# A separate choice for head 0, and an earlier start for GpSimd's gathers

## The reference

```
q = (xc @ w_q).reshape(PEER_CHUNK, PEER_HEADS, PEER_DKEY)      # 128 tokens, 8 heads, 256
s1 = q[..., :128] . keys1;  s2 = q[..., 128:] . keys2          # 128 keys each
v1, i1 = top_k(s1, 16);  v2, i2 = top_k(s2, 16)
cand = v1[:, None] + v2[None, :];  sv, si = top_k(cand, 16)
idx = e1 * 128 + e2                                            # 16 experts of 16384
g = softmax(sv)
a = gelu(u_tab[idx] . xc)
out = sum over heads and k of (g * a) * v_tab[idx]
```

## Time and profile before

| what | value |
|---|---|
| runs | 2523.37 us median of 3 (2520.69 to 2524.76) |
| profiled execution | 2523.2 us |
| its span, first to last instruction | 2521.4 us |
| VectorE, GpSimd, TensorE busy | 1533.2, 1488.0, 1406.7 us |
| read from HBM | 936.46 MB |
| the gathers' share of the 16 DMA engines | 80.7% |
| mean granted TensorE clock | 0.741 of full speed |

### The profile page before, as it was taken

One profiled execution on the slowest core, in us unless ns is written; L12 is line 12 of the kernel. 1 busy time (PEld: TensorE's weight loads), 2 busy tenths in 40 slices (PEclk: granted clock), 3 DMA queues, 4 the chain that ended last, 5 costly groups with the idle time before them and its releaser, 6 DMA issues.

```text
span 2521.4 us, 22041 instructions
## 1 busy us (share of the span) xinstructions
PE 1406.7 (56%) x7198; PEld 633.2 (25%) x7198; DVE 1533.2 (61%) x3968; ACT 344.2 (14%) x695; POOL 1488.0 (59%) x1546
## 2 busy tenths in 40 slices
PE   7897775455674665345435433369657546434333
PEld 3446521123331432011011110026434224101000
DVE  1244867877955675766776554414769755687542
ACT  2221210122301111010001000014113111000000
POOL 0001666776776567776777667610366766677773
PEclk9898887677797877667555765679869778665566
DMA  9824999999999999999999999993799999999997
GB/s 346 313 100 180 391 406 407 409 407 374 407 394 408 405 404 407 409 409 407 406 409 409 403 402 409 385 342 121 291 406 409 406 407 405 409 393 409 410 409 269
DMA packets 287856, 939.02 MB, mean 372 GB/s; under 512 B 27760, under 2 KB 28544, under 8 KB 287488
## 3 DMA queue, kind: packets, MB, share of 16 engines
q0 software_dynamic: 221184, 805.40, 80.7%
q1 hardware_dynamic: 66560, 132.21, 14.2%
HBM read 936.46 MB, written 1.05 MB: 372 GB/s over the span
## 4 chain that ended last, share of the span: by engine, by line
DMA 30%; POOL 25%; PE 24%; issue 10%; DVE 8%; ACT 2%; SPq 0%; DVEq 0%; POOLq 0%; ACTq 0%
POOL RING L720 25%; DMA RING<-in_p_v,IDV 22%; PE acc L1281 7%; DMA RING<-in_p_u,IDX 6%; PE wk L1482 5%; DVE RING L804 3%; PE wk L1343 3%; PE wk L1467 2%; PE wk L1310 1%; PE wk L1267 1%; PE wk L1320 1%; DMA WR<-in_o_w_in 1%; DVE STM L972 1%; PE wk L1426 1%; DMA WR<-in_ada_w 1%
## 5 line engine op out<-in xcount | busy, mean ns | idle before, releaser
L804 DVE SCALAR_TENSOR_TENSOR RING<-RING,acc 128x1024 f32<-128x1024 f32 x768 | 916.0, 1219 | 496.5 <-DMA RING<-in_p_u,IDX 453.4
L1281 PE MATMUL acc<-RING,ST 128*32 128x512 f32 x3072 | 604.2, 927 | 944.8 <-DMA RING<-in_p_v,IDV 942.6
L720 POOL DMA_INDIRECT RING<-in_p_u,IDX x768 | 740.3, 964 | 621.0 <-DVE WG L1072 348.2
L720 POOL DMA_INDIRECT RING<-in_p_v,IDV x768 | 746.1, 972 | 394.2 <-issue 206.8
L1281 PEld LDWEIGHTS acc<-RING,ST 128*32 128x32 f32 x3072 | 118.8, 145 | 1330.5 <-issue 1318.3
L1482 PE MATMUL wk<-HT,WR 128*128 128x256 f32 (+1 forms) x832 | 158.1, 349 | 13.1 <-DMA WR<-in_p_w_q 12.4
L1482 PEld LDWEIGHTS wk<-HT,WR 128*128 128x128 f32 x832 | 138.8, 197 | 37.6 <-issue 22.3
L1240 ACT ACTIVATE GA<-A 128x16 f32<-128x16 f32 x48 | 10.3, 215 | 739.6 <-DVE RING L804 739.5
L1343 PE MATMUL wk<-WR,HT 128*128 128x512 f32 x232 | 106.2, 614 | 2.5 <-DMA WR<-in_o_w_in 2.5
L1514 PE MATMUL wk<-SELW,WE 128*128 128x512 f32 x96 | 70.6, 825 | 41.0 <-DVE WE L825 41.0
L1242 ACT ACTIVATE ST<-wk 128x512 f32<-128x512 f32 x48 | 28.7, 597 | 375.1 <-PE wk L1514 375.1
(11 more groups left out here) (189 smaller groups left out, 1637.5 us busy)
## 6 DMA issues: line engine op xcount, KB each, us to landing
WR<-in_p_w_q SPq DMA_DIRECT2D x25, 1024.0 KB, 11.8
WR<-in_ada_w SPq DMA_DIRECT2D x23, 1024.0 KB, 11.3
RING<-in_ada_w SPq DMA_DIRECT2D x23, 1024.0 KB, 13.6
RING<-in_p_u,IDX POOLq DMA_INDIRECT x768, 11.9
RING<-in_p_v,IDV POOLq DMA_INDIRECT x768, 11.9
WR<-in_o_w_in SPq DMA_DIRECT2D x11, 1024.0 KB, 15.7
WR<-in_e_w_in SPq DMA_DIRECT2D x8, 1024.0 KB, 15.6
WR<-in_o_w_out SPq DMA_DIRECT2D x5, 1024.0 KB, 12.5
```

Of the source, the lines that this page charges most:

```text
L720: pool.indirect_dma_start(out=ring[:, n % NU, :], out_offset=None, in_=tables[table], in_offset=bass.IndirectOffsetOnAxis(ap=rows, axis=0) ...
L804: nc.vector.scalar_tensor_tensor(out=U[:, s % NU, :], in0=U[:, s % NU, :], scalar=1.0, in1=acc[:, 1, :], op0=ALU.mult, op1=ALU.mult, accum ...
L1281: ins = nc.tensor.matmul(acc[32 * g:32 * g + 32, 0, hf * 512:hf * 512 + 512], ST[:, c % 2, s, :], V[:, s % NV, hf * 512:hf * 512 + 512], s ...
```

## The change

HEAD_FIRST becomes true. The front of each layer now scores head 0, makes the "xin" transposes, makes all three parts of head 0's choice, scores head 1, makes parts 0 and 1 of its choice, scores heads 2 and 3, and goes on as before. Part 2 of head 1's choice comes after the first four products, its "ixT" one step later and its "ixD" two. The parts of the choice of (2, 3) come one step later each. GpSimd waits for a new semaphore, indexed, which the cast to IDX releases, and the cast now stands ahead of the expansion and of the wait for the exponential.

```diff
--- before.py
+++ after.py
@@ -56,7 +56,7 @@
 PAIR01 = 9
 ORDER = ((2, 3, 0, 1), (0, 1))
 ALONE = (False, True)
-HEAD_FIRST = False
+HEAD_FIRST = True
 
 
 def units(l):
@@ -135,7 +135,9 @@
     t = ORDER[l][0]
     heads = choices(l, t)[0]
     s = [("score", l, tiles, heads), ("xin", l, t), *[("topk", l, t, heads, p) for p in range(3)]]
-    return s + [("score", l, tiles, (1,))] * HEAD_FIRST + [("score", l, tiles, (2, 3)), *then]
+    if HEAD_FIRST:
+        s += [("score", l, tiles, (1,)), ("topk", l, t, (1,), 0), ("topk", l, t, (1,), 1)]
+    return s + [("score", l, tiles, (2, 3)), *then]
 
 
 def next_choices(f, l, t):
@@ -144,11 +146,10 @@
     put(f, 0, ("ixT", l, t, heads[0]))
     put(f, 1, ("ixD", l, t, heads[0]))
     if HEAD_FIRST:
-        put(f, 0, ("topk", l, t, (1,), 0), ("topk", l, t, (1,), 1))
-        put(f, 1, ("topk", l, t, (1,), 2))
-        put(f, 2, ("ixT", l, t, (1,)))
-        put(f, 3, ("ixD", l, t, (1,)))
-        choose(f, l, t, (2, 3), (2, 3, 4, 5, 6))
+        put(f, 0, ("topk", l, t, (1,), 2))
+        put(f, 1, ("ixT", l, t, (1,)))
+        put(f, 2, ("ixD", l, t, (1,)))
+        choose(f, l, t, (2, 3), (1, 2, 3, 4, 5))
     else:
         choose(f, l, t, (2, 3), (0, 1, 2, 3, 4))
 
@@ -567,6 +568,7 @@
         topks = [s[:4] for s in named("topk") if s[4] == 0]
         shifted = Count(sem("shifted"), topks)
         texp = Count(sem("texp"), topks)
+        indexed = Count(sem("indexed"), topks)
         chosen = Count(sem("chosen"), topks)
         scores_used = Count(sem("scores_used"), topks)
         u_in = [sem(f"u_in{i}") for i in range(NU)]
@@ -741,7 +743,7 @@
                     _, l, tile, h, q = s
                     c = chunk0(l, tile) + h
                     if q == 0:
-                        pool.wait_ge(chosen.sem, chosen.at(*choice(l, tile, h)))
+                        pool.wait_ge(indexed.sem, indexed.at(*choice(l, tile, h)))
                         if c > 32 * l:
                             turned(l, c - 1)
                     for s_ in range(4 * q, 4 * q + 4):
@@ -1062,11 +1064,12 @@
                         after()
                         op(nc.vector.tensor_reduce(out=IF[:, hs, :].rearrange("p h k -> p (h k)"), in_=oh3, axis=AX.X, op=ALU.add))
                         after()
+                        op(nc.vector.tensor_copy(IDX[:, par, cols], IF[:, hs, :].rearrange("p h k -> p (h k)")),
+                           indexed.sem, indexed.at(*name))
                         op(expand(IE[:, heads[0] // 2 % 2, hs, :], IF[:, hs, :], nh))
                         dve.wait_ge(texp.sem, texp.at(*name))
                         op(nc.vector.tensor_reduce(out=SM[:, hs], in_=sv, axis=AX.X, op=ALU.add))
                         after()
-                        op(nc.vector.tensor_copy(IDX[:, par, cols], IF[:, hs, :].rearrange("p h k -> p (h k)")))
                         op(nc.vector.reciprocal(SM[:, hs], SM[:, hs]))
                         after()
                         op(nc.vector.tensor_tensor(WG[:, par, cols].rearrange("p (h k) -> p h k", k=TOPK), sv,
```

## The result

The changed kernel takes 2533.20 us (median of 7 runs, 2528.30 to 2536.87), the kernel before 2523.37 (7 runs, 2518.47 to 2527.00). The ratio is 1.0036, 95% interval [1.0027, 1.0046]. The profiled execution took 2530.8 us, its span 2529.0 against 2521.4 before.

What follows compares the result with a forecast made beforehand. The time was taken as bytes over the DMA rate, about 400 GB/s, plus losses in the two layer fronts. Layer 0's +0.3 and layer 1's +1.4 us made +1.7 on 2523.2, given as 2525 us, range 2514 to 2536.

Steps and rivals of the forecast that it cites:

- its likeliest case: Whole run: within 5 us of no change, 2525 us given, own range 2519 to 2528; chance 0.47.
- rival (c): The wait behind the o_w_in products reaches the end: 8.6 us in layer 1, 2.5 in layer 0, 2534; chance 0.28.
- The single choice: Both fronts: choosing for head 0 alone takes 9.5 us, so first gathers start 13.9 and 10.6 us earlier.
- Layer 0: First product 2.5 us late behind ("adaD", 1, 3), weighed against earlier weights; layer +0.3 us, between -3.7 and +5.
- The gain: Layer 0: weights of heads 4 and 5 land near 243 instead of 251, moving 5.2 us of DMA time earlier.
- Layer 1's first product: Layer 1 front: products wait for the later ("ada", 1, 11) load and start at about 1797.2 instead of 1795.84.
- The wait for the exponential: Layer 1, after product 4: VectorE waits 8 to 11 us for head 1's exponential behind o_w_in, going on at 1815.5.
- How much of it reaches the end: Layer 1: of row 16's gather being 8.6 us late, +1.4 us reaches the end, between -3.8 and +9.
- holes of over 5 us after 1827: Layer 1: DMA engines showing such holes would mean the forecast is wrong.
- (a): Both layers: the ledger's gains count and the holes do not come, together -6.5 us, 2516.7; chance 0.20.
- (b): Both layers: the start of the gathers sets everything, -13.9 and -10.6 us, 2498.7; chance 0.05.
- The turn-taking rule: Layer 1: DMA engines alternate between queues with work, keeping +1.4 us; weights going first would give -2.

Runs made afterwards that it cites:

- e5: The changed kernel with part 2 of head 1's choice in layer 1 placed right behind the scores of heads 2 and 3; ratio to the kernel before 1.0018.
- e6: e5 and e4 together: part 2 early in layer 1, and the early block loads in free slots; ratio to the kernel before 1.0023.
- e13: The changed kernel with, in layer 1, head 1's part 2 early and both last ada blocks ahead of heads 2 and 3's projections; ratio to before 1.0037.
- e1: The changed kernel with the single choice for head 0 in layer 0 only, layer 1 keeping the pair; ratio to the kernel before 0.9998.
- e10: The same kernel as e1, run again for a finer reading; ratio to the kernel before 1.0012.
- e4: The changed kernel with layer 1's head 0 block loaded early into free v ring slots, so ada blocks keep their former slots; ratio to before 1.0059.
- e8: e6 with the ada and o_w_in steps that hold up the first products moved behind them in both layers; 2519.28 us, ratio to before 0.9985.
- the four kernels above: e5, e6, e13 and the changed kernel, whose row 16 gathers came 9.5, 9.6, 12.2 and 14.4 us later than in the kernel before.
- group A: The measurements of e5 to e9 and e13, in which the kernel before takes 2522.7 and 2520.7 us.
- group B: The measurements of e1 to e4 and three later follow-ups including e10 and e12, in which the kernel before takes 2719.4 to 2719.6 us.
- e9: The kernel before, with pairs kept, and the same steps moved behind the first products as in e8; 2530.43 us, ratio to before 1.0032.
- e3: The kernel before with only GpSimd's start at the early cast, pairs kept in both layers; ratio to the kernel before 1.0009.
- e12: e1 with ("ada", 1, 3) moved behind the first products, head 1's part 2 early and the ixT steps moved; ratio to the kernel before 1.0037.

## Why the prediction was right in its range and wrong in its likeliest case

I gave 2525 us, 2514 to 2536, and 0.28 for slower; 2533.2 is in the range and it is slower, by rival (c), which said 2534. Step by step, in the time of the kernel before:

- **The single choice**: right. First gathers 215.8 and 1777.6 forecast, 216.0 and 1777.7 measured (213.54 + 2.5, 1775.63 + 2.1). (The pair's cast ends 6.3 us after part 1, not 6.1; no term changes by it.)
- **Layer 0**: right. First product 243.4, measured 242.7 (240.15 + 2.5); row 16's gather 264.6, measured 263.8; the layer +0.3 us, measured +0.4. The gain was there too: the products of heads 4 and 5 began at 245.0 (before 251.06, forecast 243). At M0 + 120 both kernels had moved the same, 34.1 and 34.0 MB. But e5, e6 and e13 have the same layer 0 front and took 1569.2, 1569.3 and 1569.8 us from M0 to M1, so 0.4 may be a lucky trace, and the layer may cost up to 3 us. e1 and e10 could not tell.
- **Layer 1's first product**: the path was right, its length mis-sized: 1797.2 against 1804.6. This is the term that failed first, in three parts. The projections of heads 2 and 3 ended 4.9 us later than before, not 2.9, so that the second half of ("ada", 1, 11) was asked for at 1784.5 (1782.39 + 2.1), not 1782.1. Its load took 14.40 us and not 11.9, and landed at 1798.9, not 1794. From there to the first product it was 5.7 us and not 3.2: TensorE had stood for 9.35 us, and its granted clock was then 0.50, the lower of its levels (1.2 GHz).

```profile
1785.00:1796.00 11.00, 1.66 (x8) 0.23 (x8) 0.00 (x0) 0.60 (x1) 0.25 (x1) 0.70 1.03 397
1796.00:1806.00 10.00, 9.44 (x33) 5.43 (x30) 3.82 (x9) 0.60 (x1) 1.68 (x2) 0.50 1.05 381
```

The same products in the kernel before, where the clock from 1784 to 1792 was 0.93:

```profile
1787.47 1.07 PE L1310 MATMUL wk<-WR,SIL 128*32 128x512 f32 x8 [0.19 <-DMA WR<-in_ada_w]
1788.46 1.95 PE L1320 MATMUL wk<-SEL,QS 128*128 128x2 f32 x16
```

They took 1.94 and 3.58 us in the changed kernel, together 2.5 more, which is the whole of the last part.

I had also not followed the slot planner: head 0's block lost its ring slots, and so both ada blocks were asked for after M1. That was a mistake in the account, but not what made the product late: with before's slots (e4, e6) it came at +46.7 and +47.4, against +47.0.

- **The wait for the exponential**: right in kind, wrong in time. 8 to 11 us forecast, 8.43 measured; VectorE goes on at 1815.5 forecast, 1821.2 measured. I had set that moment by the landing of the last o_w_in block, with one block's 3.9 us behind it. In the trace it is TensorE's: its four o_w_in blocks could start only behind the late ada products, at 1802.28, and take 15.98 us on the chain, with no row for a load among them.
- **How much of it reaches the end**: the rule was right, the term was mis-sized. I wrote that each us beyond 1814 is a us of the run, and stood at 1815.5 with +1.4. At 1821.2 the same rule gives +7.1; layer 1 lost 9.7. What the rule had too large is the lateness of row 16's gather that costs nothing: about 8 us by my sum, about 4 by the four kernels above. The holes of over 5 us after 1827 that I had named as the sign of a wrong forecast are there: 51 GB/s from 1830 to 1835.

```profile
1830.00:1835.00 5.00, 0.00 (x0) 0.00 (x0) 4.93 (x12) 0.00 (x0) 2.26 (x3) 0.50 0.21 51
```

VectorE is busy in all of it (4.93 of 5 us) and GpSimd starts only three gathers: after the wait comes a block of choice work with no product in it, and the ring is empty of requests. The kernel before went through the same work with gathers in reserve.

- **Rival (c)** gave 8.6 in layer 1 and 2.5 in layer 0. Measured were 9.7 and 0.4 in the first pair of traces: its sum was nearly right, its split was not, so that the closeness of its 2534 is in part luck.
- **Rivals (a) and (b)**: what the earlier gathers bring to the ledger in layer 1 is 0.2 MB (2.3 less the 2.1 that the slots had left over), 0.5 us, where (a) had 3.8 us and (b) 10.6. e8 says the same from the other side: row 16's gather 13.7 us earlier and the layer no shorter.
- The turn-taking rule of the Trainium skill, "DMA: Bandwidth & Descriptors", Queues, rings and completion order: the trace fits it. A block of the ada weights among eight gathers took 14.40 us where it took 7.83 with none. That speaks against weights first; turns and plain order of arrival are not told apart by it.

Not settled: what layer 0's change costs by itself, to better than some 3 us, and why e8 is faster. Not tried: e8's layer 0 with before's layer 1 in group A, which the stretches put at about 2520 us (my estimate, 2522.7 less 3.1).

## What to carry to other kernels

In a kernel bound by a stream of transfers, an idle valley can be filled by weights or by gathers, whichever can be asked for there; bringing the gathers forward only pays if the weights that filled the valley are not pushed into the stream and if the engine that frees the buffers does not come to a stop behind them. Count bytes left at the first moment of steady flow: here it gave the length of layer 1 in seven kernels within 3 us, which the start of the first gather did not. And when a block is kept in use longer, follow the allocator: here it moved three later loads. Then ask whether they went from one idle stretch into another, in which case, as in e4 and e6, giving the slots back brings nothing.

## What the hardware showed that I had not expected

The same kernel takes 2522.7 us in group A and 2719.4 in group B, 7.8% more. Whether that is the chip is not known: the record has chip 6 beside both times (e5 to e9, e1 to e4), and chips 4 and 0 beside one of each. Group B is not slower throughout. The slices of its e3, GB/s in 40 slices of 68 us, reach 408 like group A's, and fall to 293 to 350 in others while the DMA engines are shown busy for 8 or 9 tenths:

```profile
DMA  9816999998999898999999999991998999899997
GB/s 350 307 63 255 391 395 408 352 373 293 325 394 383 327 363 339 371 368 386 371 364 377 397 408 382 383 338 63 391 360 298 361 408 383 340 349 365 375 374 279
```

Waits there are often put down to something outside the core, a releaser that no trace of group A has; in e12, for one:

```profile
238.37 0.17 DVE L1084 CAST IDV<-wk 128x16 uint32<-128x16 f32 x1 [3.56 <-remote]
```

That another user took bandwidth at that time is what this looks like; no run here shows it.

Also new to me is how short the reserve is. A ring of 8 rows is 4.2 MB, 10.7 us of the stream at 393 GB/s. In the changed kernel VectorE ended its fourth product at about 1807.2 and began its fifth at 1819.7, 12.5 us later, and the slice at 51 GB/s followed.
